# Gated attention on Trainium2: another order of units and queries, and of what waits for the stores

## The chip, the cores and the metric

The kernel runs on one core of one Trainium2 chip. The time is the device time of a run in microseconds (us); less is better. Three runs of the kernel before have a median of 3279.71 us (3278.63 to 3280.97).

## What is computed

Two transformer blocks run one after the other on 1024 tokens of width 1024, in float32. The first is a gated delta rule with a squared-ReLU MLP. The second runs an attention and, beside it, a bidirectional gated linear attention over 256 context tokens and the 1024 tokens; both are mixed by one product and followed by a gated MLP. The change lies mostly in the gated linear attention of the second block:

```python
def hgrn2_prep(q, i, f, lb_d):
    fg = lb_d + (1.0 - lb_d) * jax.nn.sigmoid(f.astype(jnp.float32))
    qh = sh(jax.nn.silu(q.astype(jnp.float32)) * (HG_HEAD_DIM ** -0.5))
    return qh, sh(1.0 - fg), sh(i.astype(jnp.float32)), sh(jnp.log(fg))

def gla_chunked(q, k, v, logf, s0):
    # S_t = diag(f_t) S_{t-1} + k_t v_t^T, o_t = S_t^T q_t
...
        A = jnp.einsum('bhtk,bhsk,bhtsk->bhts', qc, kc, decay)
        o = jnp.einsum('bhts,bhsv->bhtv', A, vc) + jnp.einsum('bhtk,bhkv->bhtv', qc * jnp.exp(b), S)

def readout(o_f, o_b, g):
        o = rmsnorm(o_f + flip(o_b), gain).reshape(Bn, T, HG_WIDTH)
        return (o * jax.nn.silu(g.astype(jnp.float32))).astype(g.dtype)
```

q is the query, i the values, f a gate for each direction (forward and backward), g an output gate. There are four heads of width 128.

## The kernel before

Every engine runs a program written out by hand; semaphores (`Signal`) connect them. A float32 product is made of three passes, with weights and inputs split into a high and a low part. A *unit* is a weight tile of 128 x 1024; all units stand in one list (`unit_list`). SyncE loads them into three buffers (`sp_weights`, L474), ScalarE writes the high part (`act_weights`, L484), the vector engine (DVE) the low part (`dve_weights`, L492), each three units ahead of the product.

**The attention** (`*_attend`) ends on every engine with `after_attend`, which waits for the ends of all engines' work and for the stores of the result to memory.

**The gated stage** (`*_gla`) goes over heads h = 0 to 3. Each needs five units: 10+h (values, "i"), 14+h and 18+h (gates f of both directions, "f" and "b"), 6+h (queries, "hq") and 22+h (output gate, "g"). The units 10 to 21 also cover the context; a unit is eight k, each in two pieces (steps), and a k takes 6 products of 128x512 and, with context, 3 of 128x256. These products are *side work* (`GlaSide`, `gla_projections`): the main chain of a head calls `side.fill(n)`, which emits n steps of it on every engine, and `side.until(x)`, which emits steps until x is there. `side.stage` says how far the side work may run ahead. The values are also turned to token order (`to_tokens`: transposes L2880, emptied by ScalarE in L2930); the emptying of the other units is L2913. After the last unit the side work goes on to the mix of both attentions (`mix_steps`): `mix_tile(k)` splits tile k of the heads' results (ScalarE L1316, DVE L1322), `mix_piece` is 4 or 2 products (L503). The first block uses the same `mix_steps` in its last head, beside a delta chain.

The main chain of a head, in the order of the tensor engine (PE):

1. The diagonal product (L2345, 16 products of 128x128) needs "kk", the sum of both keys. DVE makes it: it scales the queries (L2522), then scales each gate (L2525) and makes its key (L2527), and adds the keys (L2529).
2. Seven levels (L2358, 16 products each). Before level 0 DVE multiplies queries by gates (L2535, event "q0"), and for each level ScalarE copies a pair of keys (L2470, L2473), DVE and GpSimd (POOL) update keys, queries and gates of one direction each (L2489, L2496, L2499), and DVE copies the level's part through a mask (L2511).
3. For each direction the keys are turned (L2370) and multiplied by the values (L2376), and DVE scans the states (L2558).
4. The output (L2385 to L2387), copied by DVE (L2567) and squared by ScalarE; column sums on PE (L86), their mean (L2570), the root on ScalarE (L2454), the reciprocal (L2572), and a row product on PE (L79). DVE scales the output (L2578, L2580), and SyncE stores it (L2320, event `glast`).

The next head's L2522 waits for that store, since its queries go to the same buffer.

The last tile of the mix is split in halves (L1329, L1334) and multiplied in L1362.

## Time and profile before

| | |
|---|---|
| median of three runs | 3279.71 us |
| profiled execution | 3279.44 us |
| its span, first to last instruction | 3277.5 us |
| mean granted PE clock, share of full | 0.978 |
| PE busy | 3067.6 us, 94% |
| DVE busy | 1554.8 us, 47% |
| ScalarE busy | 997.3 us, 30% |
| GpSimd busy | 449.7 us, 14% |

The page's chain that ended last runs 82% of the span through PE, 10% through DVE and 4% through ScalarE. The gated stage lies between 1965 and 2442 us of the span, the mix of the first block between 680 and 752. A busy PE may still run at half its clock; the granted clock says so.

### The profile page before, as it was taken

The numbers are of one execution on the slowest core, as the hardware profiler recorded it, in microseconds if no ns is written. First come the engines' busy times: TensorE is split into PE (matmuls) and PEld (weight loads), VectorE is DVE, ScalarE is ACT, GpSimd is POOL, SyncE is SP. The second block draws the span as 40 slices with busy tenths as digits, with TensorE's granted clock in tenths as the row PEclk, the third lists the DMA queues.
The fourth block names the chain that finished last, engine by engine and source line by source line (L and its number), as shares of the span: only waits on it lengthen the run. The fifth ranks groups of instructions, "written<-read, shape, count | busy, mean of one in ns | idle before, by whom it ended". The sixth has DMA issues, their size and how long they took to land.

```text
span 3277.5 us, 36131 instructions
## 1 busy us (share of the span) xinstructions
PE 3067.6 (94%) x14927; PEld 2498.6 (76%) x14927; DVE 1554.8 (47%) x1919; ACT 997.3 (30%) x1435; POOL 449.7 (14%) x352
## 2 busy tenths in 40 slices
PE   7899999989899999999879999989788999999997
PEld 5788888868688888888756657877677788888886
DVE  7566666653565453433556662465463322222223
ACT  5555555542311112213323332222232211111111
POOL 4333333321000001003000001233121000000001
PEclk9999999999999999999989999999999999999999
DMA  3111111112233431112110001011121111111111
GB/s 121 39 46 46 46 46 46 46 65 97 71 116 116 124 121 49 48 52 84 53 39 9 9 11 44 14 38 39 45 97 39 45 52 45 52 45 52 45 45 58
DMA packets 77236, 184.75 MB, mean 56 GB/s; under 512 B 7057, under 2 KB 29073, under 8 KB 77073
## 3 DMA queue, kind: packets, MB, share of 16 engines
q1 hardware_dynamic: 77072, 182.44, 17.5%
q8 instruction: 119, 1.95, 0.3%
q14 instruction: 45, 0.36, 0.0%
HBM read 163.87 MB, written 15.79 MB: 55 GB/s over the span
## 4 chain that ended last, share of the span: by engine, by line
PE 82%; DVE 10%; ACT 4%; issue 2%; DMA 1%; POOL 0%; POOLq 0%; SPq 0%; DVEq 0%; ACTq 0%
PE ps L503 37%; PE ps L1552 18%; PE ps L2870 8%; PE ps L2218 4%; DVE b L2819 2%; PE ps L2358 2%; PE ps L2186 1%; PE ps L2211 1%; PE ps L2210 1%; PE ps L900 1%; DVE b L492 1%; ACT b L484 1%; PE ps L907 1%; PE ps L86 1%; DVE b L1655 1%
## 5 line engine op out<-in xcount | busy, mean ns | idle before, releaser
L503 PE MATMUL ps<-b 128*128 128x512 f32 x6024 | 1498.2, 399 | 48.0 <-DVE b L1322 15.0
L503 PEld LDWEIGHTS ps<-b 128*128 128x128 f32 x6024 | 1110.0, 190 | 265.4 <-issue 27.9
L1552 PE MATMUL ps<-b 128*128 128x512 f32 x2592 | 599.1, 392 | 0.7 <-DVE b L1687 0.7
L1552 PEld LDWEIGHTS ps<-b 128*128 128x128 f32 x2592 | 485.0, 187 | 109.3 <-DVE b L1687 1.1
L492 DVE TENSOR_TENSOR b<-b 128x1024 fp32r<-128x1024 f32 (+1 forms) x206 | 254.7, 1238 | 334.9 <-ACT b L484 328.1
L484 ACT ACTIVATE b<-b 128x1024 fp32r<-128x1024 f32 (+1 forms) x206 | 215.0, 1045 | 535.5 <-PE ps L1552 427.6
L2870 PE MATMUL ps<-b 128*128 128x512 f32 (+1 forms) x1464 | 332.1, 382 | 12.5 <-DMA scratch<-b 7.1
L2870 PEld LDWEIGHTS ps<-b 128*128 128x128 f32 x1464 | 258.8, 194 | 63.4 <-issue 17.6
L1601 ACT ACTIVATE b<-ps 128x1024 f32<-128x1024 f32 x54 | 55.4, 1026 | 378.4 <-PE ps L503 378.4
L1391 POOL TENSOR_TENSOR b<-b 128x1024 f32<-128x1024 f32 x18 | 43.2, 2398 | 908.5 <-ACT b L1422 908.1
L2218 PE MATMUL ps<-b 128*128 128x512 f32 x320 | 163.0, 592 | 0.0
L1703 DVE TENSOR_TENSOR b<-b,ps 128x1024 f32<-128x1024 f32 x64 | 78.1, 1220 | 151.7 <-PE ps L1552 151.6
L2229 ACT ACTIVATE b<-ps 128x512 f32<-128x512 f32 x160 | 95.3, 597 | 149.8 <-PE ps L2211 149.7
L1607 ACT ACTIVATE b<-b 128x1024 fp32r<-128x1024 f32 x54 | 57.3, 1061 | 260.8 <-DVE b L1682 216.6
L1705 DVE SCALAR_TENSOR_TENSOR b<-ps,b 128x1024 f32<-128x1024 f32 x48 | 61.6, 1284 | 150.2 <-PE ps L1552 150.2
L1684 DVE TENSOR_TENSOR b<-b 128x1024 f32<-128x1024 f32 x32 | 39.2, 1225 | 173.0 <-ACT b L1601 173.0
L2242 DVE TENSOR_REDUCE b<-ps 128x1 f32<-128x1280 f32 x64 | 95.3, 1490 | 47.1 <-PE ps L2186 46.7
L1229 POOL TENSOR_TENSOR b<-b 128x256 f32<-128x256 f32 x96 | 82.6, 864 | 198.9 <-DVE b L1117 115.6
L1682 DVE TENSOR_TENSOR b<-b,ps 128x1024 f32<-128x1024 f32 x22 | 26.9, 1222 | 166.2 <-PE ps L503 162.5
L2819 DVE SCALAR_TENSOR_TENSOR b<-b 128x1024 f32<-128x1024 f32 x72 | 105.3, 1463 | 0.8
L2210 PE MATMUL ps<-b 128*128 128x512 f32 x160 | 98.5, 615 | 0.0
L1687 DVE TENSOR_TENSOR b<-b 128x1024 fp32r<-128x1024 f32 x54 | 66.2, 1225 | 60.8 <-ACT b L1607 60.8
(305 smaller groups left out, 3297.4 us busy)
## 6 DMA issues: line engine op xcount, KB each, us to landing
b<-in_down SPq DMA_DIRECT2D x52, 512.0 KB, 3.6
b<-in_mod SPq DMA_DIRECT2D x96, 256.0 KB, 2.7
b<-in_gu SPq DMA_DIRECT2D x44, 512.0 KB, 3.6
b<-scratch SPq DMA_DIRECT2D x38, 512.0 KB, 4.5
b<-in_dn_in SPq DMA_DIRECT2D x32, 512.0 KB, 5.0
b<-in_up SPq DMA_DIRECT2D x32, 512.0 KB, 3.7
b<-in_win SPq DMA_DIRECT2D x26, 512.0 KB, 4.0
scratch<-b SPq DMA_DIRECT2D x18, 512.0 KB, 2.9
```

Of the source, the lines that this page charges most:

```text
L484: e.activation(self.whi[j % SPL][:, 0:cols], self.raw[j % RAW][:, 0:cols], ACT.Copy).then_inc(*self.wh.up(j))
L492: e.tensor_tensor(self.wlo[j % SPL][:, 0:cols], self.raw[j % RAW][:, 0:cols], self.whi[j % SPL][:, 0:cols].bitcast(F32), ALU.subtract).the ...
L503: ins = e.matmul(ps[:, c], w, h[:, k, c], start=first and k == 0 and i == 0, stop=last and k == KT - 1 and i == 2)
L1229: e.tensor_tensor(out, own, m.broadcast_to([128, 4, 64 >> lv, 1 << lv]), ALU.mult).then_inc(*G.up("m", h, lv, f))
L1552: ins = e.matmul(ps[:, c], w, u[:, at[k], c], start=k == 0 and p == 0, stop=k == n - 1 and p == 2)
L1703: e.tensor_tensor(x, x, ps, ALU.add).then_inc(*V.up("down", f, i))
L2210: e.matmul(S[t % 3], blk(self.ks[g], b), self.qs[g][:, :, qc], start=True, stop=False)
L2218: e.matmul(O[i % 2], self.vx[:, b, 64 * g:64 * g + 128], self.prob[(t - 2) % 4], start=b == 0, stop=b == 9).then_inc(*P.up("pv", t - 2))
L2229: e.activation(self.prob[t % 4], S[t % 3], ACT.Exp, scale=0.125).then_inc(*A.up("ex", t))
L2242: e.tensor_reduce(mx[:, j:j + 1], MX, AX.X, ALU.max).then_inc(*V.up("mx", i, j))
L2819: e.scalar_tensor_tensor(out=dst, in0=k.d_pad[c % 2][:, t:t + T], scalar=cw[:, t:t + 1], in1=dst, op0=ALU.mult, op1=ALU.add).then_inc(*V.u ...
L2870: ins = e.matmul(self.bank[p], (hi, hi, lo)[i], x, start=k == 0 and i == 0, stop=last)
```

## The change

- The units of a head are taken in another order: gates, queries, values, output gate. The values are asked for only before step 3.
- `after_attend` is gone from PE, ScalarE, DVE and POOL at the end of the attention; SyncE calls it before it loads the masks, ScalarE before it empties the first gate's unit.
- DVE makes the gates and kk without waiting for the queries and for the last head's store; the queries' product (q0) comes before it waits for the diagonal. The queries are no longer scaled; the scale is applied where the values are emptied (L2930).
- A one-element square root (`act_roots`) is added ahead of each root of a head, and of the last one of the kernel.
- `mix_steps` emits tiles 0 and 1 and three steps without a piece before the first piece.
- In head 3, `gla_fill` takes n - n/5 steps in place of n/2.

```diff
     for h in range(4):
-        units += [("win", i, 1024) for i in (10 + h, 14 + h, 18 + h, 6 + h, 22 + h)]
+        units += [("win", i, 1024) for i in (14 + h, 18 + h, 6 + h, 10 + h, 22 + h)]
...
 def mix_steps(on):
 
     on.mix_tile(0)
+    yield None
+    on.mix_tile(1)
+    yield None
+    yield None
     for k in range(KT - 1):
-        if k + 1 < KT - 1:
+        if 0 < k < KT - 2:
             on.mix_tile(k + 1)
...
         while side.stage < 4 * h - 5:
             yield "idle"
-        yield from side.to_tokens(("win", 10 + h))
-        side.ready.add((h, "i"))
         for d, n in enumerate("fb"):
             yield from side.project(("win", 14 + 4 * d + h))
...
         side.ready.add((h, "hq"))
         while side.stage < 4 * h:
             yield "idle"
+        yield from side.to_tokens(("win", 10 + h))
+        side.ready.add((h, "i"))
         yield from side.project(("win", 22 + h))
...
+    def act_roots(self, e, A):
+
+        e.wait_ge(*A.last())
+        e.activation(self.st[:, 24:25], self.con("eps", 1), ACT.Sqrt).then_inc(*A.up())
...
@@ sp_attend
-        self.after_attend(e)
+        self.sp_weights(e, UNIT["win", 14] + 4)
@@ pe_attend, and in the same way act_attend, dve_attend, pool_attend
-        self.after_attend(e)
@@ sp_gla
         V = self.gs[2]
+        self.after_attend(e)
         e.dma_start(self.masks, self.a["masks"]).then_inc(*self.maskl.up("gla"))
-        j0 = UNIT["win", 10]
+        j0 = UNIT["win", 14]
@@ gla_fill
-        return n if h < 3 else n // 2
+        return n if h < 3 else n - n // 5
@@ pe_gla
             e.wait_ge(*V.at("kk", h))
+            e.wait_ge(*A.at("ev", ("win", 6 + h), 1))
...
                 side.fill(self.gla_fill(h, self.GLA_FILL))
+            side.until((h, "i"))
             for n in "fb":
@@ gla_into
             n = "fb"[part - 2]
+            if u == ("win", 14) and c.start == TC:
+                self.after_attend(e)
...
             if h:
+                e.wait_ge(*P.at("dg", h - 1))
                 e.wait_ge(*V.at("q0", h - 1))
@@ act_gla
             side.fill(self.gla_fill(h, 6))
+            self.act_roots(e, A)
             e.wait_ge(*V.at("oms", h))
@@ dve_gla
         for h in range(4):
-            side.stage = 4 * h
-            side.until((h, "hq"))
             f = {n: B[f"f{n}{h % 2}"] for n in "fb"}
             k, q = {"f": B["kf"], "b": B["kb"]}, {"f": B["qf"], "b": B["qb"]}
-            e.wait_ge(*A.at("ev", ("win", 6 + h), 1))
-            if h:
-                e.wait_ge(*self.glast.at(h - 1))
-                e.wait_ge(*G.at("up", h - 1, 6))
-            e.tensor_scalar(B["hq"], B["hq"], 128.0 ** -0.5, None, ALU.mult)
+            side.stage = 4 * h
+            side.until((h, "b"))
             for d, n in enumerate("fb"):
                 j = 4 * d + h
+                e.wait_ge(*A.at("ev", ("win", 14 + j), 2))
...
             e.tensor_tensor(B["sq"], k["f"][:, TC:TA], k["b"][:, TC:TA], ALU.add).then_inc(*V.up("kk", h))
+            side.until((h, "hq"))
+            e.wait_ge(*A.at("ev", ("win", 6 + h), 1))
+            if h:
+                e.wait_ge(*self.glast.at(h - 1))
+                e.wait_ge(*G.at("up", h - 1, 6))
+            for n in "fb":
+                ins = e.tensor_tensor(q[n], B["hq"], f[n][:, TC:TA], ALU.mult)
+            ins.then_inc(*V.up("q0", h))
             side.fill(self.gla_fill(h, 8))
             e.wait_ge(*P.at("dg", h))
             side.fill(self.gla_fill(h, 3))
             put(self.con("ident"), D0, "put", h, "d")
-            for n in "fb":
-                ins = e.tensor_tensor(q[n], B["hq"], f[n][:, TC:TA], ALU.mult)
-            ins.then_inc(*V.up("q0", h))
@@ act_last
         P, A, V, G = self.mm2
+        self.act_roots(e, A)
         e.wait_ge(*V.at("ms2"))
@@ ActSide.turned
-                         ACT.Copy).then_inc(*self.sig[1].up("tv", u, j))
+                         ACT.Copy, scale=128.0 ** -0.5).then_inc(*self.sig[1].up("tv", u, j))
```

Two places show how instructions move. The first is DVE where head 3 begins. Before, in rows from the kernel before:

```order
L2580 SCALAR_TENSOR_TENSOR b<-b 128x1024
L2522 TENSOR_SCALAR b<-b 128x1024
L2525 TENSOR_SCALAR b<-b 128x1280
L2527 TENSOR_SCALAR b<-b 128x1280
L2525 TENSOR_SCALAR b<-b 128x1280
L2527 TENSOR_SCALAR b<-b 128x1280
L2529 TENSOR_TENSOR b<-b 128x1024
L492 TENSOR_TENSOR b<-b 128x1024
L2511 COPY_PREDICATED b<-b,ps 128x1024
L2535 TENSOR_TENSOR b<-b 128x1024 x2
```

After, with the changed kernel's line numbers (L2595 is the L2580 of before, L2534 to L2538 are L2525 to L2529, L2545 is L2535, L501 is L492, L2524 is L2511, L2502 is L2489):

```order
L2595 SCALAR_TENSOR_TENSOR b<-b 128x1024
L2534 TENSOR_SCALAR b<-b 128x1280
L2536 TENSOR_SCALAR b<-b 128x1280
L2534 TENSOR_SCALAR b<-b 128x1280
L2536 TENSOR_SCALAR b<-b 128x1280
L2538 TENSOR_TENSOR b<-b 128x1024
L2545 TENSOR_TENSOR b<-b 128x1024 x2
L501 TENSOR_TENSOR b<-b 128x1024
L2524 COPY_PREDICATED b<-b,ps 128x1024
```

The scaling of the queries is gone, and the queries' product stands right behind kk, ahead of the split of a unit and of the mask copy that waits for the diagonal.

The second is PE in the first block's last head, where the mix begins. Before (L870 and L888 belong to the delta chain and stand there for both halves, L503 is the mix):

```order
L865 MATMUL ps<-b 128x128 x8
L870 MATMUL ps<-b 128x128 x4
L503 MATMUL ps<-b 128x512 x4
L870 MATMUL ps<-b 128x128 x4
L503 MATMUL ps<-b 128x512 x4
L888 MATMUL ps<-b 128x128 x4
L503 MATMUL ps<-b 128x512 x2
L888 MATMUL ps<-b 128x128 x4
L503 MATMUL ps<-b 128x512 x2
L882 MATMUL ps<-b 128x128 x2
L900 MATMUL ps<-b 128x128 x2
```

After (L879 is L870, L897 is L888, L512 is L503, L891 and L909 are L882 and L900):

```order
L874 MATMUL ps<-b 128x128 x8
L879 MATMUL ps<-b 128x128 x8
L897 MATMUL ps<-b 128x128 x8
L512 MATMUL ps<-b 128x512 x4
L891 MATMUL ps<-b 128x128 x2
L909 MATMUL ps<-b 128x128 x2
L512 MATMUL ps<-b 128x512 x4
L891 MATMUL ps<-b 128x128 x2
L909 MATMUL ps<-b 128x128 x2
```

The first mix products now stand behind both halves of L870 and L888, where they stood between the halves.

## Rows read from the trace of the kernel before

**Rows 1.** The page, part 1: busy time, share of the span, instructions.

```profile
PE 3067.6 (94%) x14927; PEld 2498.6 (76%) x14927; DVE 1554.8 (47%) x1919; ACT 997.3 (30%) x1435; POOL 449.7 (14%) x352
```

**Rows 2.** Waits of PE, 1955 to 2445 us: total, times, longest.

```profile
PE ps L2345 <- DVE b L2529: 18.5, 4, 8.3
PE ps L79 <- DVE b L2572: 7.3, 3, 2.4
PE ps L2870 <- DMA scratch<-b: 7.1, 1, 7.1
PE ps L2358 <- DVE b L2535: 6.4, 4, 2.5
PE ps L503 <- DVE b L1322: 5.4, 1, 5.4
PE ps L2870 <- ACT b L2930: 4.2, 4, 1.9
```

**Rows 3.** Windows, head by head: width, busy time of each engine, clock, DMA.

```profile
1965.30:2030.00 64.70, 63.15 (x302) 52.71 (x302) 9.71 (x10) 14.38 (x21) 0.00 (x0) 0.96 0.18 56
2030.00:2126.00 96.00, 89.37 (x543) 78.77 (x543) 48.90 (x58) 27.62 (x43) 28.46 (x21) 0.98 0.04 12
2126.00:2236.00 110.00, 97.13 (x579) 85.40 (x578) 57.49 (x65) 30.36 (x46) 30.40 (x21) 0.97 0.09 29
2236.00:2344.00 108.00, 100.08 (x582) 87.67 (x581) 56.50 (x65) 29.13 (x45) 28.83 (x21) 0.95 0.09 30
2344.00:2442.00 98.00, 71.19 (x399) 60.73 (x398) 63.74 (x75) 25.51 (x35) 30.43 (x21) 0.88 0.18 60
```

**Rows 4.** Timeline, 1950 to 2005 us: start, duration, instruction, idle time before.

```profile
1965.36 16.48 PE L2870 MATMUL ps<-b 128*128 128x512 f32 x72 [7.08 <-DMA scratch<-b]
...
1969.06 1.23 DVE L492 TENSOR_TENSOR b<-b 128x1024 fp32r<-128x1024 f32 x1 [6.64 <-DMA b<-in_masks]
```

**Rows 5.** Timeline where head 3 begins.

```profile
2344.19 2.98 PE L2870 MATMUL ps<-b 128*128 128x512 f32 x12
...
2347.04 0.33 SPq L2320 DMA_DIRECT2D scratch<-b  x1
...
2350.05 0.69 DVE L2522 TENSOR_SCALAR b<-b 128x1024 f32<-128x1024 f32 x1 [3.04 <-DMA scratch<-b]
...
2355.49 3.78 PE L2345 MATMUL ps<-b 128*128 128x128 f32 x16 [8.33 <-DVE b L2529]
```

**Rows 6.** Timeline, ScalarE: the root's table and the root.

```profile
2124.00 1.28 ACT L2454 ACT_TABLE_LOAD   x1
...
2432.68 1.28 ACT L2454 ACT_TABLE_LOAD   x1
...
2434.06 0.21 ACT L2454 ACTIVATE b<-b 128x8 f32<-128x8 f32 x1
```

**Rows 7.** Timeline in levels of heads 0 and 3; durations (min/median/max) of L2489.

```profile
2053.21 4.76 PE L2870 MATMUL ps<-b 128*128 128x512 f32 x23
...
2057.81 1.95 PE L2358 MATMUL ps<-b 128*128 128x128 f32 x16
...
2368.81 2.16 PE L2358 MATMUL ps<-b 128*128 128x128 f32 x16 [0.81 <-POOL b L2496]
...
2375.82 2.97 PE L2358 MATMUL ps<-b 128*128 128x128 f32 x16 [3.46 <-DVE b L2511]
...
L2489 POOL TENSOR_TENSOR b<-b x28: 1277/1442/3124, 2037.6 to 2393.9; 128x640 f32<-128x640 f32 x28
```

**Rows 8.** Timeline where the first block is mixed.

```profile
688.88 2.04 PE L503 MATMUL ps<-b 128*128 128x512 f32 x4 [9.60 <-DVE b L1322]
...
752.26 47.99 PE L503 MATMUL ps<-b 128*128 128x512 f32 x211
```

**Rows 9.** Timeline at the end of the gated stage.

```profile
2435.51 1.03 PE L79 MATMUL ps<-b 128*128 128x128 f32 x8
...
2439.36 1.48 DVE L1334 TENSOR_TENSOR b<-b 128x512 fp32r<-128x512 f32 x2
```

More of the change, by code:

```diff
@@ L2229, in act_attend @@
             e.activation(self.prob[t % 4], S[t % 3], ACT.Exp, scale=0.125).then_inc(*A.up("ex", t))
-        self.after_attend(e)
     def dve_attend(self, e):
@@ L2283, in dve_attend @@
                 shift(i + 1)
-        self.after_attend(e)
     def pool_attend(self, e):
@@ L2294, in pool_attend @@
             e.tensor_copy(self.qx[g][r], self.qs[g][r, :, qc].bitcast(F32)).then_inc(*G.up("qx", i))
-        self.after_attend(e)
     GLA_ORDER = {"f": list(range(9)), "b": [1, 0, 9, 8, 7, 6, 5, 4, 3]}
@@ L2438, in act_gla @@
                 side.fill(self.gla_fill(h, self.GLA_FILL))
+            side.until((h, "i"))
             for n in "fb":
@@ L2544, in dve_gla @@
                 side.fill(self.gla_fill(h, self.GLA_FILL))
+            side.until((h, "i"))
             for n in "fb":
```

## The prediction

> **What bounds the kernel now.** I read the page first: the tensor engine (PE) is busy 94% of the span [rows 1], so an edit pays only where it takes idle time or slow clock from PE, since no product is added or dropped. Then the list of PE's waits, cut to the gated stage (1955 to 2445 us): its 16 lines add up to 63.4 us, and the six largest carry 49 of it [rows 2]. The reader should see whose line ends each: the stage's first product waits 7.1 for the stores of the attention; four diagonal products wait 18.5 for the vector engine (DVE, L2529); four first levels wait 6.4 for the queries' product (L2535); three row products wait 7.3 for the reciprocal of a root; the mix waits 5.4 once for its low half. Then the windows by head, for the granted clock [rows 3]: 0.96, 0.98, 0.97, 0.95 and 0.88. Width times what is missing from 1.00 is 2.6, 1.9, 3.3, 5.4 and 11.8, together 25 us of lost clock, part of it while PE stands anyway. The lower level (half, 1.2 GHz) comes where PE stood idle just before; the last head, with the most idle time (71 busy of 98), has the lowest clock. The timeline gave the rest [rows 4 to 9].
>
> The sum is made against the profiled execution: 3279.44 us, a span of 3277.5 and 1.9 around it, 0.3 under the median of the three runs (3279.71), so no correction is needed.
>
> **Yardsticks.** A 512-wide product costs 47.99/211 = 0.227 us [rows 8]. 23 side products take 4.60 from start to start [rows 7]: 15 wide ones make 3.41, so a 256-wide one costs (4.60 - 3.41)/8 = 0.149. A unit with context (48 wide, 24 narrow) is thus 14.5 us, one without 10.9. A level's 16 products take 1.95 each time, 1.7 of it before the next group starts [rows 7].
>
> **The edits one by one.**
>
> (a) No wait for stores. PE's last attention product ends at about 1958.3, the first gated one starts at 1965.36 [rows 4]. Its weights lie ready, since the first two units were split before the attention. The new wait for the stores stands in ScalarE, before it writes the first gate: that is one unit (14.5 us) after 1958.3, at about 1973, and the stores are through at 1965. DVE still stands until the masks land (its L492 at 1969.06 [rows 4]); that is the split of the third unit, needed two units (29 us) after 1958.3, so it stays hidden. Gain 7.1.
>
> (b) Values behind the gates, first head. One unit of 14.5 us leaves the stretch before the diagonal, with its two token waits of 0.6 and 0.8, and the gates come earlier. In head 0 the second gate is there at about 1987, kk 5 us after its splits at about 1994, q0 at about 2003; PE reaches the diagonal at 2006 and the first level at 2010. Its waits there (1.5 for kk, 1.8 for q0, in the totals of [rows 2]) go, with the two token waits: gain 4.7.
>
> (c) Heads 1 to 3, the diagonal. In head 3 the rows end at R = 2344.19, the store is issued at R + 2.85, DVE scales the queries only at 2350.05 because it waits for that store, and kk ends 5.4 later [rows 5]. After, the gates' chain is not behind the store and has no scaling: it starts at R + 2.9 and takes 5.4 - 0.6 = 4.8, so kk is there at R + 7.7. PE now has 36 side products of the values (24 wide, 12 narrow, 7.2 us) instead of 12 to 28 wide ones; in head 2 there is one more step, in head 3 only 32 products (6.4). Waits left: 0.4, 0 and 1.2. Before they were 5.6, 3.0 and 8.3 (the 8.3 is in [rows 5]; with head 0's 1.5 they are the 18.5 of [rows 2]). Gain 15.4.
>
> (d) Queries' product ahead of the diagonal: q0 is there 2.4 after kk, and PE needs 1.7 for the diagonal and 2.5 to 3 for side products before the level. The waits of 4.6 left of the 6.4 [rows 2] go. The store has landed by then. Gain 4.6.
>
> (e) Tokens of the values now turn in the early levels, where ScalarE has to copy a key pair (waiting for DVE and GpSimd) before it empties the turned tokens. I take 1.2 in each of three heads and 4.0 in head 3, where the turning stands directly behind its unit, and 1.5 for three emptyings of the last query gate behind a table load: 9.1, against 5.8 such waits before (3.4 of them in [rows 2], which also holds head 0's 0.8 of (b)). Loss 3.3; bounds, 5.8 gained if none shows, 9 lost if heads 0 to 2 look like head 3.
>
> (f) Levels. Between levels 1 and 3 DVE and GpSimd have more to do than PE has filler in heads 0 to 2: GpSimd's keys take 1.44 as a rule and 3.12 at most, and PE waited 3.46 for such a level in the starved last head [rows 7]. I take 1.4 a head, 4.1 in all, against 6.5 now (nearly all in head 3, which now gets 120 unit products of filler where it had 48). Gain 2.4; bounds, 6.5 gained and 14 lost (two waits of 3.46 in each of three heads, 20.8).
>
> (g) End of head 3. The mix wait of 5.4 shrinks to about 2.3, since both splits now stand behind the last mask instruction; of 2.6 + 0.8 + 0.7 for scans and the ninth transpose I leave 1.7. But the side work ends earlier: the chain from the rows' end (2435.51 + 0.8) to the low half of the last tile (2439.36 + 0.75) is 3.8 us [rows 9], covered now by 20 side products and then by 8 small ones only, 0.9: loss 3.0. Net gain 2.5.
>
> (h) Root's table loaded ahead. The load already runs before its activation has its input: in head 3 it stands at 2432.68 to 2433.96 and the root at 2434.06 [rows 6]. In heads 0 to 2 the load directly follows ScalarE's emptying of a product (2124.00 [rows 6]), which the edit leaves in front of it. So it brings 0 and the added one-element activation 0.2 in each of three heads: loss 0.6; bounds, 0 and 4 x 1.28 gained. The Trainium skill, "ScalarE: Activation LUTs", What ACT_TABLE_LOAD costs, gives 1283 ns for the load and 1380 ns of drain, 2.66 us a switch, which would make a wrongly placed load worth 8 us in three heads; the trace agrees on the load (1.28) and shows no such drain ahead of the root.
>
> (i) Mix tiles earlier, also in the first block's last head. PE stands 9.6 us for the first low half [rows 8]; DVE gets to it no sooner. But 12 small products that stood behind the stall now run inside it (1.7 us), and 8 wide ones now stand before a late 0.9 us wait. Gain 2.6 (from 0 to 5).
>
> (j) Clock. Of the 25 us, the stretch behind the stores' wait goes whole (2.6), head 3 loses most of its idle time; I take half, 12.5, back. Bounds: 5 and 20.
>
> Sum: 7.1 + 4.7 + 15.4 + 4.6 - 3.3 + 2.4 + 2.5 - 0.6 + 2.6 + 12.5 = 47.9. 3279.4 - 47.9 = 3231.5, **3232 us**.
>
> **Rivals.**
>
> Main case, as above, 0.62; its own range 3222 to 3244.
>
> The levels take over (0.17). With less filler, DVE and GpSimd set the pace. For: the 3.46 of [rows 7]. Against: three quarters of the levels keep 3.2 us and more of filler. If two levels in each of three heads wait 3.46, that is 21 us: 3253. The Trainium skill, "GPSIMD Engine Reference", Specifications, says that GpSimd shares its memory interfaces with VectorE and contends when that one has two inputs from memory; it would give this case. The trace agrees that both engines' times stretch (the same keys take GpSimd 1.44 as a rule and 3.12 at most).
>
> More comes back (0.12): the token and level waits of (e) and (f) don't appear (13 us less) and the clock stays up (5 more): 3214.
>
> The stage's start gains nothing (0.05): the first unit stands for another wait at the same place (its split weights, or ScalarE for the stores). 7.1 and 2.6 fall away: 3242.
>
> Not faster (0.04): every level takes the 7.0 us that level 1 to 2 took in head 3 (2368.81 to 2375.82 [rows 7]). With 5.5 us a level in heads 0 to 2 (1.7 and 14 to 23 side products) and 4.4 in head 3 (1.7 and mostly 12) that is 21 x 1.5 + 7 x 2.6 = 50, and idle PE halves the clock for some 5 more: 3287. It decides from 1.7 us of extra wait a level.
>
> **Chances.** A difference under 0.2% (6.6 us) can't be told from none. Faster 0.95, the same 0.02, slower 0.03. The range takes in the main case, the start's rival and most of the levels': 3217 to 3252.
>
> **What the new profile would show.** Right: no wait for a DMA at the stage's start, the first gated product at about 1956 (1958.3 less the gain of (i)); no diagonal wait over 1.5; DVE's product of the queries done before PE's diagonal; the three row waits still 2.4 to 2.7; a new wait of 2 to 4 us at the last mix (L1362's line); head 3's window above 0.93. Wrong: waits of 3 us at level products, or turned tokens held up by over 2 us in heads 0 to 2; the clock at half in every head; row waits fallen to about 1, which would mean that the load did stand behind its wait.

## The result, and the profile after

The changed kernel takes 3224.26 us (median of 4 runs, 3223.74 to 3225.72), the kernel before beside it 3279.17. The ratio is 0.9832, with a 95% interval from 0.9817 to 0.9848: 55 us or 1.7% faster. The forecast was 3232, in a range from 3217 to 3252. The profiled execution took 3223.74, with a span of 3222.0, which is 55.5 less than the 3277.5 before; the accounts below are made between these two spans.

First the page of the changed kernel, part 1: busy time, share of the span, instructions.

```profile
PE 3057.1 (95%) x14927; PEld 2493.4 (77%) x14927; DVE 1556.7 (48%) x1915; ACT 997.9 (31%) x1440; POOL 450.8 (14%) x352
```

The matmuls are the same in number, and they are busy 10.5 us less [rows 1]. No product was dropped: a product at the lower clock counts longer, so this is the clock's part.

The list of PE's waits in the gated stage (1950 to 2390 us of the changed kernel) answers to [rows 2]. It is the whole list: total, times, longest.

```profile
PE ps L79 <- DVE b L2587: 7.6, 3, 2.5
PE ps L2886 <- ACT b L2946: 5.9, 4, 2.3
PE ps L2365 <- ACT b L2486: 3.2, 3, 1.7
PE ps L79 <- issue: 3.1, 1, 3.1
PE ps L512 <- DVE b L1331: 2.5, 2, 2.1
PE ps L2896 <- ACT b L2929: 1.5, 1, 1.5
PE ps L2378 <- DVE b L2524: 0.8, 1, 0.8
PE ps L2378 <- DVE b L2573: 0.8, 1, 0.8
PE ps L2886 <- ACT b L2929: 0.5, 1, 0.5
```

It adds up to 25.9 us. The 16 lines of before add to 62.6 (the prediction wrote 63.4, an addition slip that no term used). The lines for the stores, for the diagonal's sum (L2538 now) and for the queries' product (L2545 now) are gone whole. The largest line left is the one for the three row products, 7.6. The line "issue" is the 3.1 us ahead of the last row product.

The windows of the changed kernel, head by head, answer to [rows 3] (width, busy time of each engine, clock, DMA):

```profile
1953.00:2091.40 138.40, 133.45 (x763) 115.61 (x761) 61.54 (x68) 37.24 (x57) 29.83 (x21) 1.00 0.12 35
2091.40:2192.70 101.30, 96.34 (x576) 85.00 (x576) 56.45 (x64) 30.19 (x47) 30.96 (x21) 0.98 0.10 32
2192.70:2293.00 100.30, 95.06 (x576) 83.73 (x576) 56.88 (x64) 29.69 (x46) 29.90 (x21) 1.00 0.10 32
2293.00:2385.50 92.50, 81.35 (x485) 70.77 (x485) 66.11 (x76) 29.35 (x43) 30.62 (x21) 0.96 0.19 63
```

Width times the missing clock is now 0, 2.0, 0 and 3.7, together 5.7 us, where it was 25. And the last head holds 485 products, where it had 399 [rows 3]: a unit more of side work falls into its waits, and into less time (92.5 us, where it was 98).

Four places of the timeline of the changed kernel: where the first block is mixed (against [rows 8]), where the stage begins (against [rows 4]), where head 3 begins (against [rows 5]), and the end (against [rows 9]).

```profile
678.99 1.04 PE L874 MATMUL ps<-b 128*128 128x128 f32 x8
...
681.67 0.66 PE L879 MATMUL ps<-b 128*128 128x128 f32 x4 [0.57 <-DVE b L1126]
683.08 0.66 PE L897 MATMUL ps<-b 128*128 128x128 f32 x4 [0.75 <-DVE b L1135]
685.39 0.65 PE L897 MATMUL ps<-b 128*128 128x128 f32 x4 [1.65 <-DVE b L1135]
690.71 2.04 PE L512 MATMUL ps<-b 128*128 128x512 f32 x4 [4.66 <-DVE b L1331]
...
1950.74 2.74 PE L2227 MATMUL ps<-b 128*128 128x512 f32 x6
...
1952.91 22.45 PE L2886 MATMUL ps<-b 128*128 128x512 f32 x113
...
1960.40 1.28 ACT L2929 ACT_TABLE_LOAD   x1 [7.79 <-DMA scratch<-b]
...
2293.93 8.06 PE L2886 MATMUL ps<-b 128*128 128x512 f32 x32
...
2300.32 1.23 DVE L2538 TENSOR_TENSOR b<-b 128x1024 f32<-128x1024 f32 x1
2301.47 2.35 DVE L2545 TENSOR_TENSOR b<-b 128x1024 f32<-128x1024 f32 x2
2301.82 1.95 PE L2352 MATMUL ps<-b 128*128 128x128 f32 x16
...
2384.68 1.06 PE L79 MATMUL ps<-b 128*128 128x128 f32 x8 [3.14 <-issue]
```

The stall of 9.60 at the first low half is 4.66, but it is not shorter by the difference: it is broken up. Twelve small products (three rows of x4) now stand inside it and wait 0.57, 0.75 and 1.65 themselves, so PE stands 7.6 us in all. The first mix product comes 11.72 us after the products of L874; before, it came 11.71 after the same ones (L865, at 677.17). PE walks from the attention's last product into the gated stage without a wait, and the stores' wait now stands in ScalarE (7.79 us at 1960.40), where nothing needs it. In head 3 the sum of the gates ends at 2301.55, R + 7.6 (R = 2293.93, the end of the rows, where the side products begin, as in the prediction), and the diagonal begins 0.3 later with no wait shown: the sum came just in time, under 32 side products that took 7.9 us from their start to the diagonal's. DVE's product of the queries begins 0.35 before the diagonal and ends with it.

### The profile page after: what moved, and what is told of

Read it like the earlier page. It is cut to its first block, busy times and chain, and to the rows that moved or that the text cites. A ratio compares the mean times of both kernels' runs of the same rounds, so it can differ in the third digit from the quotient of the medians.

```text
span 3222.0 us, 36124 instructions
## 1 busy us (share of the span) xinstructions
PE 3057.1 (95%) x14927; PEld 2493.4 (77%) x14927; DVE 1556.7 (48%) x1915; ACT 997.9 (31%) x1440; POOL 450.8 (14%) x352
## 3 DMA queue, kind: packets, MB, share of 16 engines
q8 instruction: 119, 1.95, 0.3%
## 4 chain that ended last, share of the span: by engine, by line
PE 85%; DVE 8%; ACT 4%; issue 2%; DMA 0%; POOL 0%; SPq 0%; POOLq 0%; DVEq 0%; ACTq 0%
PE ps L512 38%; PE ps L1561 18%; PE ps L2886 9%; PE ps L2227 4%; DVE b L2835 2%; PE ps L2365 1%; PE ps L2195 1%; PE ps L909 1%; PE ps L2220 1%; PE ps L2219 1%; DVE b L501 1%; ACT b L493 1%; PE ps L916 1%; PE ps L86 1%; PE ps L891 1%
## 5 line engine op out<-in xcount | busy, mean ns | idle before, releaser
L512 PE MATMUL ps<-b 128*128 128x512 f32 x6024 | 1498.5, 400 | 40.1 <-DVE b L501 13.6
L512 PEld LDWEIGHTS ps<-b 128*128 128x128 f32 x6024 | 1111.2, 190 | 258.2 <-issue 19.2
L501 DVE TENSOR_TENSOR b<-b 128x1024 fp32r<-128x1024 f32 (+1 forms) x206 | 255.4, 1241 | 298.8 <-ACT b L493 291.9
L2886 PEld LDWEIGHTS ps<-b 128*128 128x128 f32 x1464 | 257.1, 193 | 57.0 <-issue 11.6
```

The source lines that it names most:

```text
L501: e.tensor_tensor(self.wlo[j % SPL][:, 0:cols], self.raw[j % RAW][:, 0:cols], self.whi[j % SPL][:, 0:cols].bitcast(F32), ALU.subtract).the ...
L512: ins = e.matmul(ps[:, c], w, h[:, k, c], start=first and k == 0 and i == 0, stop=last and k == KT - 1 and i == 2)
L2886: ins = e.matmul(self.bank[p], (hi, hi, lo)[i], x, start=k == 0 and i == 0, stop=last)
```

## The experiments

Twelve kernels were run, in three sets of four, each set on one chip beside the kernel before (medians 3279.65, 3280.34 and 3280.56 there). Undoings are of the changed kernel; f1 and c1 are built on the kernel before. The waits and the last column come from one profiled execution of each kernel.

| kernel | edit | us median (range) | ratio to before, 95% | PE waits in the stage | the rest |
|---|---|---|---|---|---|
| before | | 3279.17 | 1 | 62.6 | 1583.4 |
| changed | | 3224.26 | 0.9832 (0.9817 to 0.9848) | 25.9 | 1533.0 |
| a0_changed | again | 3224.82 (3219.92 to 3228.95) | 0.9831 (0.9816 to 0.9846) | 26.0 | 1533.6 |
| u1_stores | stores' wait back | 3235.88 (3231.28 to 3239.56) | 0.9864 (0.985 to 0.9879) | 33.5 | 1547.3 |
| u2_roots | no root ahead | 3222.55 (3220.81 to 3229.32) | 0.9828 (0.9812 to 0.9844) | 25.8 | 1533.5 |
| u3_mix1 | first block's old mix | 3231.30 (3230.01 to 3232.31) | 0.9851 (0.9836 to 0.9866) | 26.0 | 1533.5 |
| u4_query | product behind diagonal | 3235.30 (3231.07 to 3237.05) | 0.9859 (0.9844 to 0.9874) | 34.3 | 1542.3 |
| u5_values | values ahead of gates | 3246.87 (3243.72 to 3248.30) | 0.9897 (0.9883 to 0.9912) | 38.4 | 1553.8 |
| u6_fill3 | halved fill in head 3 | 3233.56 (3231.86 to 3235.64) | 0.9856 (0.9841 to 0.9871) | 31.7 | 1543.0 |
| f1_order | units' order alone | 3273.47 (3271.23 to 3278.22) | 0.998 (0.9971 to 0.9989) | 56.5 | 1577.9 |
| c1_busy | extra products in waits | 3281.59 (3276.41 to 3287.33) | 1.0001 (0.9992 to 1.0011) | 48.9 | 1583.7 |
| p1_rows | as u2, more fill asked for | 3224.80 (3222.78 to 3225.91) | 0.9828 (0.9814 to 0.9843) | 25.8 | 1533.4 |
| p3_root_first | root ahead of emptyings | 3213.26 (3210.34 to 3217.97) | 0.9793 (0.9777 to 0.981) | 19.4 | 1525.9 |
| p4_kept_steps | and steps kept for the end | 3214.30 (3212.69 to 3216.31) | 0.98 (0.9785 to 0.9814) | 18.8 | 1525.7 |

**How the last column is made, and why it is needed.** Medians of kernels that do the same work (changed, a0, u2, p1) differ here by 2 us, and single runs by more. The traces show where that comes from. Ten of these kernels do the same, instruction for instruction, up to the attention, and its first product starts between 1686.51 and 1693.63 us. Here are two of them; first the changed kernel, that product in the timeline and a window ahead of it that holds 141 products (columns as in [rows 3]):

```profile
1689.01 1.40 PE L2195 MATMUL ps<-b 128*128 128x512 f32 x3 [7.62 <-DMA b<-b]
```

```profile
1599.74:1634.68 34.94, 33.26 (x141) 26.30 (x142) 18.43 (x26) 8.53 (x14) 0.00 (x0) 0.84 0.13 34
```

and the same kernel run again (a0_changed), the same product and the window of the same 141 products:

```profile
1693.63 1.41 PE L2195 MATMUL ps<-b 128*128 128x512 f32 x3 [7.62 <-DMA b<-b]
```

```profile
1601.42:1640.87 39.45, 34.62 (x141) 27.04 (x142) 18.34 (x26) 8.54 (x14) 0.00 (x0) 0.82 0.11 30
```

The same products take 34.94 us once and 39.45 the other time. The mean clock differs little; the half-clock products stand in other places. In the changed kernel 16 and 18 of them take 3.03 and 6.47 us where a0 has 1.95 and 4.38, but a0 then waits 3.16 us for DVE, and both reach the next product 9.3 us after the first of these. Three groups that are slow in a0 (3.41, 2.91 and 2.92 us, where changed has 1.84, 1.65 and 1.88) have no such wait behind them. So I take "the rest": the span less the start of that product. Five kernels have the same work behind it, but for the roots and, in p1, the place of a few side products (changed, a0, u2, u3, p1), and their rests lie between 1533.0 and 1533.6. This measure tells 1 us, where the medians tell some 3; below, differences "in the rest" are to 1533.4, or to the 1583.4 of before.

> The changed kernel once more, on this chip, as the base of the three beside it: 3224, and its spread shows what a difference of medians is worth.

### u1_stores: the wait for the stores put back

```diff
@@ at the end of each engine's attend, five times
+        self.after_attend(e)
@@ sp_gla, gla_into
-        self.after_attend(e)
```

> The changed kernel with one edit undone: all engines wait again for the stores of the attention before the gated stage. Theory (term a is a term of its own): the 7.1 us wait is back at the stage's first product and the clock of that stretch is lower again, up to 2.6 us more: 3224.3 + 7.1 to 9.7 = 3231 to 3234. Rival (the start of the stage would stand for something else in any case, or the lead gained there is lost again at the first diagonal): 3224 to 3226.

Measured: 11.6 us more in the median, 14 in the rest. From the list of waits of this kernel:

```profile
PE ps L2888 <- DMA scratch<-b: 7.1, 1, 7.1
```

It is back with just its 7.1. All waits grew by 7.6, which leaves 6.3 of the 13.9 for slower products: the windows of the heads show 0.99, 1.00, 0.98 and 0.93. Of the 6.3, 2.3 stand right behind the wait: the stage's first 233 products take 49.9 us here and 47.6 in the changed kernel and in four others without the wait (a0, u2, u3, p1). Those behind them stand behind the same waits in both kernels: in head 3 a level behind a wait of 2.31 takes 3.57 us here, where changed has 1.95 behind 2.30. Behind the stage it is 1.4 us more than in changed, but 0.5 more than in a0. The term is real and more than its wait. The 11.6 lies above the range of 9.7 that I gave.

### u3_mix1: the first block's mix steps put back

```diff
@@ DeltaSide.projections
-        yield from mix_steps(self.on)
+        yield from mix_steps_old(self.on)      # the loop of the kernel before
```

> The changed kernel with the old order of the mix tiles in the first block alone. Theory now held (the whole lead before the attention comes from this edit): the changed kernel ends its delta stage 4.6 us earlier than the kernel before, so 3224.3 + 4.6 = 3229, and the 9.6 us wait for the low half is back. By the term of the prediction: 2.6, so 3227. Rival (the lead comes from elsewhere): 3224 to 3225.

Measured: 7.0 more in the median, and nothing in the rest (1533.5): the edit acts ahead of the attention alone. Its stall is again 9.6 us. What the edit is worth where it acts shows between two marks that every kernel has: the 8 products just ahead of the place where the mix begins (L865 before, 677.17; L874 changed, 678.99; 676.80 here) and the products behind the mix's last tile (752.26, 748.12 and 751.82). That is 75.1, 69.1 and 75.0 us for the same products; the four kernels with the old mix have 74.1 to 75.1, the ten with the new one 67.8 to 69.1. So the edit is worth 6 us. The waits between these marks tell where: those at the stall and its small products fell from 10.0 to 8.1, and the small waits of the recurrence behind it (L882, L907, L922, L936, L960 of before) from 5.2 to 1.5. What is above 6 is the stretch behind, which differs from run to run: the four kernels with the old mix reach the attention at 1694.7 on the mean (1691.47 to 1696.90), the ten with the new one at 1689.2.

### u4_query: the queries' product behind the diagonal again

```diff
@@ dve_gla
-            (waits for the store; q[n] = B["hq"] * f[n]; "q0")   # ahead of the fill of 8
             put(self.con("ident"), D0, "put", h, "d")
+            (the same lines)
```

> The changed kernel with the queries' product behind the diagonal again, its wait for the store with it. Theory (terms c and d): the diagonals don't wait, since the sum of the gates doesn't come later, but the first levels wait 1.5 to 2.5 us each for the product, as before: 4.6 to 6.4 us, and up to 2 of clock: 3229 to 3233. Rival (the side products ahead of the level cover it now): 3224 to 3226.

Measured: 11 us more in the median, 8.9 in the rest, of which 8.4 are waits. From its list:

```profile
PE ps L2365 <- DVE b L2549: 7.2, 4, 2.5
```

Each of the four first levels waits, as before the change (6.4 then). The rival falls; the side products ahead of the level don't cover it.

### u5_values: the values' unit ahead of the gates again

```diff
@@ unit_list
-        units += [("win", i, 1024) for i in (14 + h, 18 + h, 6 + h, 10 + h, 22 + h)]
+        units += [("win", i, 1024) for i in (10 + h, 14 + h, 18 + h, 6 + h, 22 + h)]
@@ gla_projections: to_tokens(("win", 10 + h)) ahead of the two gates
```

> The changed kernel with the values' unit ahead of the gates again in all four heads, everything else as changed. Theory (the vector engine's new order and the units' new order both are needed): head 0 loses 4.7 us; in heads 1 to 3 the sum of the gates is ready 7.7 us after the rows but the tensor engine has only 3 to 6 us of products for that time, so diagonal waits of about 2, 0 and 4.7 us return; the turned values cost 3.3 less; with some 2 us of clock that is 3224.3 + 4.7 + 6.7 - 3.3 + 2 = 3234. Rival (the vector engine's order alone does it): 3224.3 + 4.7 - 3.3 = 3226.

Measured: 22.6 more in the median, 20.4 in the rest, twice what I expected. The whole of it can't be read from the diagonals: their waits are 4.2. The windows of head 0 and head 3 of this kernel show the reason:

```profile
1953.00:2107.60 154.60, 149.54 (x845) 128.92 (x844) 62.95 (x69) 41.24 (x65) 28.97 (x21) 1.00 0.11 32
...
2312.90:2407.10 94.20, 72.61 (x402) 63.14 (x403) 64.20 (x74) 25.68 (x36) 32.08 (x21) 0.89 0.19 62
```

Head 0 has 82 products more than in the changed kernel (845 against 763) and takes 16.2 us longer; head 3 has 83 fewer (402 against 485) and takes 1.7 us *longer* still. One unit of side work, which in the changed order lies inside head 3's waits at no cost, stands here in heads that have no waits to fill. And the emptied head 3 has the clock of before (0.89, [rows 3] had 0.88).

### f1_order: the order of the units alone, on the kernel before

```diff
@@ on the kernel before: unit_list and gla_projections as changed
+            side.until((h, "i"))     # PE, ScalarE and DVE, ahead of the transposes
```

> The kernel before with one edit alone: the values' unit behind the gates and the queries, in the list of units and in the side work; the vector engine's order, the stores' wait, the fill of head 3 and the mix stay as before. Theory (the order of the units acts mainly by keeping a unit of 14.5 us of the last head for its waits, whatever the vector engine does): about the 22 us that undoing it cost, 3279.5 - 22 = 3257, with more products in head 3 (about 480 in place of 399) and fewer in head 0. By terms b and e of the prediction: 4.7 - 3.3, so 3278. Rival in between (it pays only where the vector engine's new order lets the gates go first): 3265 to 3272.

Measured: 7.1 us less than before, 5.5 in the rest. That is a third, at most, of what undoing it cost. Head 3 of this kernel:

```profile
2318.70:2432.00 113.30, 87.55 (x485) 74.88 (x485) 64.92 (x76) 29.21 (x42) 30.59 (x21) 0.89 0.19 63
```

It has the 485 products, but takes 113.3 us: the halved fill uses few of the side steps in its waits, and the diagonals, with the store still ahead of the vector engine's chain, wait 12.3 us in all. So my first theory falls as well as the terms' 3278: the order brings the work into head 3, and it takes more to put it into the waits there. The larger fill is one part (u6_fill3). DVE's new order is likely the other: no run has it alone, but the diagonals wait 12.3 us with the units' order and without it, 4.2 with it and the larger fill in the old order of units (u5_values), and nothing with all three. The in-between rival (3265 to 3272) is nearest, 1.5 us off.

### u6_fill3: the halved fill of head 3 again

```diff
@@ gla_fill
-        return n if h < 3 else n - n // 5
+        return n if h < 3 else n // 2
```

> The changed kernel with the old, halved share of side work in the levels of head 3. Theory (the filler in head 3 is what keeps the clock there and the levels covered): the level waits grow from 3.2 to some 6 us and the clock of head 3 falls from 0.96 to about 0.90, 5 us, while the 3.1 us wait at the last rows goes, since side work is left for it: 3224.3 + 3 + 5 - 3.1 = 3229. Rival (the same products fill later waits just as well): 3224.3 - 3.1 = 3221.

Measured: 9.3 more, 9.6 in the rest. The wait at the last rows is gone, as expected, but the first row product and the levels of head 3 wait (the first line was 7.6 in three waits, the second was not there):

```profile
PE ps L79 <- DVE b L2587: 10.3, 4, 2.6
...
PE ps L2365 <- DVE b L2524: 3.1, 1, 3.1
```

All waits grew by 5.8 and the window of head 3 has a clock of 0.92. The theory holds, its size was 5 us short.

### u2_roots and p1_rows: no root ahead

```diff
@@ act_gla, act_last
-            self.act_roots(e, A)
@@ pe_gla, p1_rows only
-            side.fill(self.gla_fill(h, 6))
+            side.fill(self.gla_fill(h, 6) + (3 if h < 3 else 0))
```

> The changed kernel without the added one-element roots (in the gated stage and in the last norm). Theory (term h): the table is loaded ahead of its root in any case, and the added activation costs 0.1 to 0.2 us in each of three heads: 3224.3 - 0.6 = 3223.7, no difference that can be measured, and the three row waits go from 2.54 back to 2.45. Rival (the load stood behind the wait for the sums): 3 to 4 times 1.28, 3228 to 3229, with row waits of 3.8.

> The changed kernel without the added roots, and with three more steps of side work in heads 0 to 2 on the tensor engine alone, between the column sums and the row products (it waits 2.54 us there in each head). Theory (the side work is there, and nothing behind it is late): the three waits of 7.6 us go nearly whole, 3224.3 - 0.6 - 6 = 3218, with a little clock 3216. Rival (the next head's diagonal then waits for the sum of the gates instead): 3223 to 3224.

Measured: 3222.55 and 3224.80, rests 1533.5 and 1533.4: no difference from the changed kernel. The row waits are 2.45 in place of 2.54. So the root's table brought nothing and cost next to nothing. p1_rows taught that more fill at that place doesn't help. In heads 0 and 1 PE's products between the column sums and the row product are the same as in u2_roots; in head 2 they are 18 in place of 14, and the row product comes 2.45 us after the last of them all the same. So the wait counts from the end of PE's side products there, not from the column sums. The theory behind it (filling takes the wait) falls.

### p3_root_first: the root ahead of the last emptyings

The trace of u2_roots shows what the row products wait for:

```profile
2082.83 3.45 PE L2884 MATMUL ps<-b 128*128 128x512 f32 x14
2083.11 0.17 DVE L2584 TENSOR_SCALAR b<-ps 128x8 f32<-128x8 f32 x1 [4.67 <-PE ps L86]
2085.64 1.28 ACT L2927 ACTIVATE b<-ps 128x512 f32<-128x512 f32 x2 [4.81 <-PE ps L2884]
2086.93 1.28 ACT L2466 ACT_TABLE_LOAD   x1
2088.23 0.21 ACT L2466 ACTIVATE b<-b 128x8 f32<-128x8 f32 x1
2088.47 0.20 DVE L2586 RECIPROCAL b<-b 128x8 f32<-128x8 f32 x1 [5.19 <-ACT b L2466]
...
2088.73 1.09 PE L79 MATMUL ps<-b 128*128 128x128 f32 x8 [2.45 <-DVE b L2586]
```

The sums are ready at 2083.28, but ScalarE stands 4.81 us for PE to end the output gate's unit, empties it, and only then loads and takes the root. Its emptyings were ahead of the root by program order alone.

```diff
@@ act_gla
-            side.fill(self.gla_fill(h, 6))
-            self.act_roots(e, A)
             e.wait_ge(*V.at("oms", h))
             e.activation(small[:, 8:16], small[:, 0:8], ACT.Sqrt).then_inc(*A.up("ort", h))
+            side.fill(self.gla_fill(h, 6))
```

> The changed kernel without the added roots, and with ScalarE's own share of side work (the last two emptyings of the output gate) behind the root in place of ahead of it. Theory (the row products wait for ScalarE, which first empties two banks, 1.28 us, then loads the table, 1.28, then takes the root): the root comes while the tensor engine still has 14 side products, the three waits of 2.45 to 2.54 go, and nothing behind them is late, since the gates' chain counts from the rows too: 3224.3 - 0.6 - 7.3 = 3216. Rival (the output gate, now behind the root with a table load of its own, holds up the vector engine, its store and so the next head's query product, and the wait shows at the diagonal or the first level): 3221 to 3224.

Measured: 3213.26, 11 us under the changed kernel, 0.9793 of before; 7.5 of it in the rest. The same place in its trace:

```profile
2082.99 1.28 ACT L2465 ACT_TABLE_LOAD   x1
...
2086.27 3.45 PE L2884 MATMUL ps<-b 128*128 128x512 f32 x14
2086.56 0.17 DVE L2584 TENSOR_SCALAR b<-ps 128x8 f32<-128x8 f32 x1 [4.67 <-PE ps L86]
2086.76 0.21 ACT L2465 ACTIVATE b<-b 128x8 f32<-128x8 f32 x1 [2.48 <-DVE b L2584]
...
2089.57 1.04 PE L79 MATMUL ps<-b 128*128 128x128 f32 x8
```

With nothing ahead of it, the load runs before the sums are there. The three waits (7.6 in the changed kernel, 7.3 in u2_roots, from which this kernel differs by the move alone) are gone, and 1.5 us of diagonal waits have come in. It beats both kernels.

### p4_kept_steps: three steps kept for the end

```diff
@@ all three engines, the levels
-                side.fill(self.gla_fill(h, self.GLA_FILL))
+                side.fill(self.gla_fill(h, self.GLA_FILL) - (h == 3 and lv in (2, 4, 6)))
@@ pe_gla, between the column sums and the row products
-            side.fill(self.gla_fill(h, 6))
+            side.fill(6 if h < 3 else 1)
```

> The kernel p3_root_first with three steps of head 3's side work taken out of levels 2, 4 and 6 and, on the tensor engine, kept for the end of the stage: 12 products stand between the two row products, where the changed kernel waits 3.1 us with nothing left to do. Theory: 12 x 0.227 = 2.7 of the 3.1 go, and the levels that lose four products each wait 0 to 1 us more in all: 3216 - 2 = 3214. Rival (the levels of head 3 need every step, as in u6_fill3): 3217 to 3219.

Measured: 3214.30, rest 1525.7, the same as p3_root_first. The wait at the last rows fell as worked out, from 3.1 to 0.4 us, and the wait for the mix's low half grew from 2.6 to 5.4:

```profile
PE ps L512 <- DVE b L1331: 5.4, 2, 4.5
```

Head 3's side work is used up; moving it moves the wait. The rival was right in kind, though not in its place: the levels didn't wait, the mix did. That 3214 was forecast is luck: it stood for 2 us less than a base of 3216, which itself came out at 3213.

### c1_busy: extra products in the waits of the kernel before

```diff
@@ pe_gla, on the kernel before
+            if h:
+                e.wait_ge(*V.at("of", h - 1, 0))
+            x = blk4(self.b_hi, 0, 0)
+            for n in range((5, 20, 11, 32)[h]):
+                e.matmul(D0[:, 0:512], x[:, 0:128], x, start=True, stop=True)
             e.wait_ge(*V.at("kk", h))
```

> The kernel before, unchanged in its order, with 5, 20, 11 and 32 extra 512-wide products put into the four diagonal waits (1.5, 5.6, 3.0 and 8.3 us) just ahead of the wait; their result is overwritten and not used. No wait is removed. Theory (the half clock follows the tensor engine's standing): the half-clock stretches behind the diagonals go and the time falls by 2 to 8 us, to 3271 to 3277, and the windows of heads 1 to 3 show a clock of 0.97 or more. Rival (the clock doesn't depend on these waits, or the extra products hold up what follows): 3279 or more, the windows as before.

Measured: 3281.59, no difference (0.9992 to 1.0011), and a rest of 1583.7 against 1583.4; the stage alone takes 476.4 us in both. The diagonal waits fell from 18.5 to 2.2, and all waits by 13.7; the 68 extra products took 15.4. The windows of head 2 and head 3:

```profile
2239.00:2346.00 107.00, 99.73 (x590) 87.23 (x591) 56.72 (x66) 29.89 (x46) 28.84 (x21) 0.98 0.10 30
2346.00:2445.00 99.00, 79.87 (x434) 67.98 (x433) 63.42 (x75) 25.54 (x35) 30.01 (x21) 0.88 0.18 59
```

Head 2 rose from 0.95 to 0.98, head 3 stayed at 0.88 with its 8.3 us wait filled. That is not the whole of it. Here is head 3 behind the diagonal's wait: the first level before (the diagonal of before, 3.78 us, is in [rows 5]),

```profile
2362.92 3.69 PE L2358 MATMUL ps<-b 128*128 128x128 f32 x16 [2.50 <-DVE b L2535]
```

and the diagonal and the first level in c1_busy:

```profile
2358.46 2.05 PE L2350 MATMUL ps<-b 128*128 128x128 f32 x16
...
2365.36 3.39 PE L2363 MATMUL ps<-b 128*128 128x128 f32 x16 [3.91 <-DVE b L2540]
```

The clock did come back right behind the filled waits: the diagonals of heads 1 to 3 took 3.57, 3.79 and 3.78 us before, and 2.05 each here. In the 9.5 us from head 3's diagonal on, the granted clock was 0.68 before and 0.92 here. But the first level can't start before DVE has the queries' product, and DVE's chain is as long as it was. So PE came sooner and stood longer: these waits grew from 6.4 to 10.1, and from the row product to the first level head 3 takes 19.6 us before and 19.7 here. The first half of my theory (the half clock behind the diagonals goes) holds, the second (the time falls by 2 to 8 us) falls. This run can't price the clock, since what it won had to be waited for.

## Why the prediction was right, point by point

Between the two spans, by the prediction's terms. (b) and (e) both had token waits; here these stand together in (e).

| term | predicted | measured | from |
|---|---|---|---|
| (a) stores | 7.1 | 7.1 | line gone; u1_stores brings back 7.1 |
| (b) head 0, diagonal and level | 3.3 | 3.3 | both lines gone |
| (c) diagonals of heads 1 to 3 | 15.4 | 17.0 | line gone |
| (d) queries' product | 4.6 | 4.6 | line gone; u4_query brings back 7.2 |
| (e) token and bank waits | 1.4 - 3.3 = -1.9 | -0.7 | 7.2 before, 5.9 + 1.5 + 0.5 after |
| (f) levels | 2.4 | 3.3 | 6.5 before, 3.2 after |
| (g) end of head 3 | 2.5 | 2.3 | 9.5 before, 2.5 + 0.8 + 0.8 + 3.1 after |
| (h) root's table | -0.6 | -0.3 | 7.3 before, 7.6 after |
| (i) first block's mix | 2.6 | 5.4 | 12.45 earlier at the stage's start, less (a) |
| (j) clock | 12.5 | 13.5 | what is left of 55.5 |
| sum | 47.9 | 55.5 | |

**Right in kind.** Each mechanism that the prediction named is in the trace, at its place: the first gated product without a wait, the diagonals without one, DVE's product of the queries ahead of the mask copy, with no level waiting for it, row waits of 2.54, and a new wait of 3.1 us at the end (I had 3.0, and named L1362's line; it shows at the row product in front of it). Head 3's window is at 0.96 (I said above 0.93). One sign of "right" is not met: DVE's product of the queries was to be done before PE's diagonal, and is so in head 0 alone. In heads 1 and 3 it begins before the diagonal and ends within it or with it, and in head 2 it ends 0.9 us behind it; the side products ahead of the level cover that. None of the signs of "wrong" is there; the turned tokens held PE 2.3 us at most, in head 3.

**Mis-sized: (i), by more than half.** The 5.4 in the table is a difference of two executions that were 1.8 us apart before the edit acts; between the two marks of u3_mix1 the edit is worth 6, outside the bounds of 0 to 5. The part that the prediction reasoned out is right: DVE gets to the low half no sooner (11.7 us behind the same products in both), and the 12 small products inside the stall take 1.9 us of waits out, where I had 1.7. Missed were the small waits of the recurrence behind the stall, which fell by 3.7, where I had counted one of 0.9. Why the recurrence waits less, once the mix's products stand elsewhere in it, no run shows.

**(c) came out 1.6 better by luck.** The chain was sized right: the sum of the gates is there at R + 7.6, where I had R + 7.7. What was off is the cover: the 32 side products of head 3 ran 7.9 us where I had 6.4, since they began at the lower clock behind the row's wait:

```profile
2293.90:2297.90 4.00, 4.00 (x16) 3.33 (x15) 3.52 (x4) 0.00 (x0) 0.00 (x0) 0.57 0.06 24
```

It is the same in head 1 (0.57 in the first 4 us), and not in head 2 (1.00). So the waits of 0.4 and 1.2 that I left didn't show because PE was slow, not because the sum was early; nothing was won by that.

**(e) and (f)** were 1.2 and 0.9 too dark; both are inside their bounds.

**(j)** came out at 13.5 by difference. By the windows, the missing clock fell by 19 (25 to 5.7), part of which PE had waited through anyway. Behind the stores' wait I had 2.6, and u1_stores shows 2.3. For the rest the prediction had the lower level come "where PE stood idle just before". The diagonals bear it out: behind waits of 3 to 8 us they took 3.6 to 3.8, behind filled or vanished ones 2.05 (c1_busy) and 1.95 (changed). What the term lacked is that clock won ahead of a bound chain becomes a wait, as in c1_busy. It counts in the changed kernel because the queries' product comes earlier there too. So the half that I took has no working behind it, and its fit is in part luck.

In head 3 the levels' own waits count as well: they are much the same in c1_busy as before (3.5 for L2511's line in both), and so is the clock of the head, 0.88. u5 and u6, where the levels of head 3 have less side work, lost 8 and 4 us of clock beside their waits, most of it in head 3 (0.89, 0.92), and f1, with the work but the halved fill, has 0.89. I read this as most of head 3's clock going with the side work among the small waits of the levels; no run here changed the one alone and kept all waits.

**What the single terms don't tell.** Undone one by one, the edits cost, in the rest, 13.9 (stores), 8.9 (query), 20.4 (values' order) and 9.6 (fill): 53 together, more than the 50.0 that the rest fell by in all, and DVE's earlier gates are not among them. The units' order alone brings 5.5, and costs 20.4 when it is taken out of the whole. The prediction booked it as head 0's gain of (b) and a loss in (e); its larger part is the work that it brings to head 3, which (c), (f) and the clock then showed as theirs. The sum was right because it went by waits, stretch by stretch; read as prices of the edits, its terms would have been wrong.

**The rivals.** Levels that take over: three level waits, 1.7 us at most. More comes back (3214): the time lies nearly half-way to it, but not by its mechanism. The token and level waits came out 2.1 us better, of its 13, and the clock 1.0, of its 5; the other gain was (i), and (c) on paper. A start that gains nothing: refuted by u1_stores. Not faster: no level waits more than 1.7 us.

**Left open.** Of the 6 us that the stores' wait costs beside its own 7.1, 2.3 stand right behind it; whether the slower products in heads 2 and 3 come from it too, or are the chance of one execution, is not shown.

## What to carry to other kernels

Where one stretch starves and its neighbours are full, look for work that may be done later: an edit of order is worth the waits that it fills, and it needs the fill counts that let it in; so price a set of edits by stretches, not one by one. When a short chain gates the bound engine (here a root), look at what stands ahead of it on its own engine, by program order alone; loading its table early cured nothing, moving two emptyings behind it took 7.3 us of waits away (1.5 came back at the diagonals). And a wait that is filled gives back clock, but the clock gives back time only where no other engine's chain sets the next start. And where single runs differ by more than the effect, subtract a stretch that the edit can't touch: it told 1 us where the medians told 3.

## What the runs showed of the hardware that was not expected

The same instructions, ahead of the attention, took up to 7 us more or less from one kernel to the next (1686.51 to 1693.63). The same 141 products took 34.94 and 39.45 us at nearly the same mean clock (0.84 and 0.82): what differed is whether the half-clock products stood ahead of a wait, where they cost nothing, or not. And behind the same row wait of 2.54 us the first 4 us were granted 0.57 in heads 1 and 3 of the changed kernel and 1.00 in head 2, so the price of one wait in clock can't be read from one place.
